# Attentions by two: both older units' value products together behind the scores of the next two

## The reference, cut to what matters

```python
# first block, per head
probs = softmax(concat([scores, sink]))[..., :-1]
out = einsum('bnkgqs,bnskd->bnqkgd', probs, v_band)
# second block: compressed, selected and window attention
p_cmp = where(valid, softmax(where(valid, q @ k_cmp, NEG_INF)), 0.0);  o_cmp = p_cmp @ v_cmp
o_slc = softmax(s) @ v_sel
o_win = softmax(s) @ v_win
return g[0] * o_cmp + g[1] * o_slc + g[2] * o_win
```

## Time and profile before

| | us |
|---|---|
| median of 3 runs | 2228.23 |
| lowest, highest | 2225.65, 2231.48 |
| profiled execution | 2233.68 |
| its span | 2231.9 |
| TensorE busy | 2207.0 (99%) |
| DVE busy | 1552.2 (70%) |
| ACT busy | 1110.0 (50%) |
| GpSimd busy | 198.4 (9%) |
| mean granted clock of TensorE | 0.998 |

### The profile page before, as it was taken

One profiled execution on the slowest core, in us unless ns is written; L12 is line 12 of the kernel. 1 busy time (PEld: TensorE's weight loads), 2 busy tenths in 40 slices (PEclk: granted clock), 3 DMA queues, 4 the chain that ended last, 5 costly groups with the idle time before them and its releaser, 6 DMA issues.

```text
span 2231.9 us, 34104 instructions
## 1 busy us (share of the span) xinstructions
PE 2207.0 (99%) x13650; PEld 1900.3 (85%) x13662; DVE 1552.2 (70%) x2163; ACT 1110.0 (50%) x1719; POOL 198.4 (9%) x191
## 2 busy tenths in 40 slices
PE   8999999999999999999999999999999999999998
PEld 7888888888888888888889988888888888998887
DVE  5777845677864775777787677567666777777764
ACT  4745434655543544445454554455444546355443
POOL 0010200001200110000004011011100000310110
PEclk9999999999999999999999999999999999999999
DMA  7445565445555755554535465565556444355553
GB/s 238 142 142 180 188 200 186 152 133 180 182 193 187 243 189 189 185 182 152 171 105 171 169 215 184 193 236 192 190 184 193 161 164 138 133 199 181 187 189 133
DMA packets 109245, 397.72 MB, mean 178 GB/s; under 512 B 12384, under 2 KB 12528, under 8 KB 108832
## 3 DMA queue, kind: packets, MB, share of 16 engines
q1 hardware_dynamic: 104256, 377.01, 50.8%
q0 software_dynamic: 4832, 18.53, 2.6%
HBM read 395.00 MB, written 1.05 MB: 177 GB/s over the span
## 4 chain that ended last, share of the span: by engine, by line
PE 96%; DVE 2%; ACT 1%; DMA 1%; issue 0%; DVEq 0%; SPq 0%; ACTq 0%; POOLq 0%
PE psum L449 44%; PE psum L600 29%; PE psum L599 15%; PE psum L818 2%; PE psum L963 2%; PE psum L940 1%; PE psum L927 1%; PE psum L898 1%; PE psum L2043 1%; PE psum L1319 0%; DMA ring<-in_weights 0%; DMA pages<-in_gains 0%; PE psum L1333 0%; ACT attn_p L1103 0%; DVE xs L2396 0%
## 5 line engine op out<-in xcount | busy, mean ns | idle before, releaser
L406 DVE TENSOR_TENSOR w_low<-ring,w_high 128x1024 fp32r<-128x1024 f32 x704 | 858.5, 1231 | 332.7 <-ACT w_high L403 331.3
L403 ACT ACTIVATE w_high<-ring 128x1024 fp32r<-128x1024 f32 x704 | 734.6, 1056 | 511.2 <-DMA ring<-in_weights 506.1
L600 PE MATMUL psum<-xT,w_high 128*128 128x512 f32 x2784 | 983.0, 397 | 0.0
L599 PE MATMUL psum<-xT,w_low 128*128 128x256 f32 x2784 | 790.3, 284 | 0.0
L600 PEld LDWEIGHTS psum<-xT,w_high 128*128 128x128 f32 x2784 | 522.8, 188 | 123.5 <-issue 1.0
L599 PEld LDWEIGHTS psum<-xT,w_low 128*128 128x128 f32 x2784 | 526.1, 189 | 3.9 <-issue 1.4
L449 PE MATMUL psum<-w_high,hidden 128*128 128x512 f32 x1216 | 376.9, 390 | 0.0
L449 PEld LDWEIGHTS psum<-w_high,hidden 128*128 128x128 f32 x1216 | 228.3, 188 | 47.2
L449 PE MATMUL psum<-w_low,hidden 128*128 128x512 f32 x608 | 236.6, 389 | 0.0
L449 PE MATMUL psum<-w_high,xT 128*128 128x512 f32 (+2 forms) x640 | 193.3, 382 | 0.7 <-DVE xT L777 0.6
L449 PE MATMUL psum<-rounded_pages,w_high 128*128 128x256 f32 x896 | 165.6, 286 | 0.0
(11 more groups left out here) (238 smaller groups left out, 2089.0 us busy)
## 6 DMA issues: line engine op xcount, KB each, us to landing
ring<-in_weights SPq DMA_DIRECT2D x706, 512.0 KB, 3.5
pages<-in_affine POOLq DMA_DIRECT2D x16, 512.0 KB, 5.5
ring<-in_weights SPq DMA_DIRECT2D x8, 440.0 KB, 3.2
pages<-in_gains POOLq DMA_DIRECT2D x4, 512.0 KB, 4.8
pages<-in_mem POOLq DMA_DIRECT2D x2, 1024.0 KB, 6.6
pages<-in_bias POOLq DMA_DIRECT2D x2, 988.0 KB, 11.8
ring<-in_weights SPq DMA_DIRECT2D x4, 384.0 KB, 3.2
pages<-in_rows POOLq DMA_DIRECT2D x2, 512.0 KB, 5.8
```

Source lines behind the costliest of these rows:

```text
L403: eng.activation(high, raw, ACT.Copy).then_inc(self.flag("w_rounded").sem, 1)
L406: eng.tensor_tensor(self.w_low[:, piece % SLOTS, 0:width], raw, high.bitcast(F32), ALU.subtract).then_inc(self.flag("w_split").sem, 1)
L599: pe.matmul(out[:, 0:SEQ], low, self.xT_high[:, k, :], start=(k == 0), stop=False, skip_group_check=True)
L600: m = pe.matmul(out, high, self.xT[:, k, :, :].rearrange("p x s -> p (x s)"), start=False, stop=(k == kn - 1), skip_group_check=True)
```

## The change

In `attend_tensor_by_two` TensorE's order changes; the other engines' orders do not. Before, the value products of unit i-2 stand behind the scores of units i and i+1, and those of unit i-1 behind the turned weights of unit i. After, both stand behind the scores. At the end, the two last units' value products both stand behind the last two steps' work, in place of one behind each.

```diff
         for i in range(0, len(us), 2):
             self.scores_of_two(pe, l, us[i])
             if i:
-                self.values(pe, l, us[i - 2])
+                for u in us[i - 2:i]:
+                    self.values(pe, l, u)
             between(i)
             self.turn_weights(pe, l, us[i])
-            if i:
-                self.values(pe, l, us[i - 1])
             between(i + 1)
             self.turn_weights(pe, l, us[i + 1])
         for i in range(2):
             between(len(us) + i)
-            self.values(pe, l, us[len(us) - 2 + i])
+        for u in us[-2:]:
+            self.values(pe, l, u)
```

## The result

| | before | after |
|---|---|---|
| median of 7 runs, us | 2226.26 | 2234.09 |
| lowest, highest | 2225.54, 2231.48 | 2232.24, 2237.32 |
| profiled span | 2231.9 | 2232.4 |

The ratio is 1.0032, 95% interval 1.0023 to 1.0041: 7.1 us slower by the ratio, 5.1 to 9.1. The forecast was +4.7, with 2232.9 for the time and 2227.5 to 2239 as its range. It called the loss a small one inside 0.3%; the interval lies on both sides of that bound, so these runs do not settle it.

What follows compares the result with a forecast made beforehand. It took TensorE's queue, 96% of the chain, to bound the kernel. Terms of -3.3 - 0.4 + 5.6 + 2.8 = +4.7 us on the median 2228.23 gave 2232.9 us, range 2227.5 to 2239.

Steps and rivals of the forecast that it cites:

- Step 1: Pairs behind the first: one break less between TensorE's matrix products gains 0.33 us per pair, 3.3 us over 10 pairs.
- Rival D: Pairs and ends: removing the break gains nothing, so 3.7 us of gain vanish; +8.4 us, 2236.6; chance 0.05.
- Step 2: DVE's copies of turned weights: in time in block 1; 0.33 us late in block 2's four branch pairs, cancelling their gain.
- Step 3: End of block 2: two value products together behind two branch products gain 0.2 us per layer, 0.4 in all.
- Step 4: First pair of block 2: V(7) waits for DVE's finish of unit 6; net +3.2 and +2.4, together +5.6 us.
- Step 5: Behind V(7)'s wait in each layer of block 2: TensorE's clock drops, 1.4 us per layer, +2.8 us in all.
- rival B: At the gate and T(8) behind V(7): low clock lasts a second stretch, 1.7 us more per layer; +8.1, 2236.3; chance 0.19.
- Rival A: First pair of block 2: the waits come but the clock holds; +1.9 us, 2230.1; chance 0.17.

Runs made afterwards that it cites:

- only where nothing should be late: Value products joined in block 1, three gate pairs of block 2 and the ends, first and branch pairs unjoined; against the kernel before: 2225.52 against 2228.74 us, ratio 0.9986.
- Short finish: Changed kernel with the last addition of the selected and window attention's finish cut to 8 columns; against the kernel before: 2234.02 against 2228.04 us, ratio 1.0023.
- branch pairs alone: Kernel before with only the two pairs of block 2 beside branch products joined; against the kernel before: 2230.74 against 2228.74 us, ratio 1.0012.
- copy ahead of the rest: Changed kernel, block 2's first pair unjoined, DVE's copy moved ahead of multiplication and weight split from the ninth unit; against the kernel before: 2222.37 against 2228.04 us.
- first pair apart: Changed kernel, but the first pair of block 2 keeps the old order; against the kernel before: 2228.4 against 2228.74 us, ratio 1.0000.
- the filler: Changed kernel with 17 idle matrix products between the value products of units 6 and 7; against the kernel before: 2230.16 against 2228.04 us, ratio 1.0010.
- First pair alone: Kernel before with only the first pair of block 2 joined; against the kernel before: 2238.68 against 2228.74 us, ratio 1.0042.
- second profiles: The kernel before and the changed kernel, both unchanged, each profiled a second time: 2229.59 and 2234.55 us.
- Before again: The kernel before, unchanged, profiled a second time: 2229.59 us.
- after again: The changed kernel, unchanged, profiled a second time: 2234.55 us.
- block 1 alone: Kernel before with only the pairs of block 1 joined; against the kernel before: 2224.6 against 2228.0 us, ratio 0.9985.

## Why the prediction came out as it did

**Right in sign, place and, nearly, size.** The bound, the waiting instruction and its releaser were named, and the time lies in the range. That the total came so near is partly luck, as the last point says. By steps:

- **Step 1, a break: right.** 0.33 per pair predicted. A gate pair of the change (T(9) to T(11), 9.02 us for 9.36) gives 0.34. A pair of block 1 gives 0.4 (T(1) to T(3), 9.30 us for 9.70). Rival D would have it 0. The Trainium skill, TensorE: Matmul & The Clock Gate, Step-by-step: what each phase is for, says that weight loads are pulled ahead of products in flight; if they were pulled across the break too, that would be rival D. These rows speak against it here, as does "only where nothing should be late" with -3.1 (-5.1 to -1.1).
- **Step 2, the copies: the term that failed.** The place was right and the size was not. It stood as 0 for the four branch pairs, "0.33 us, which cancels the gain", with a loss of 0.5 as the worst. It measured +0.85 per pair, +3.4 us, outside those bounds. I took DVE's arrival at the copy from the trace of before, where V(i-1) behind T(i) gave DVE 0.79 us more, and left out the finish. With V(i-1) gone, DVE's list between two copies is the longer one. "Short finish" (waits 0.97 to 0.45) and "branch pairs alone" show it; "copy ahead of the rest" removes it. That DVE would catch up in the wait at V(7) was right, as the 0.80 of "first pair apart" shows.
- **Step 3, the ends:** 0.2 per layer predicted, 0.34 measured (T(19) to L818, 13.21 us for 13.55).
- **Step 4, V(7): right.** A net +3.2 was predicted for layer 0 without the clock. With the filler V(6) to T(9) takes 11.69 us where before took 8.50: +3.2, in layer 1 too. There I had 2.4, 0.8 us too little. In the trace that I read, TensorE was at half clock ahead of V(6) and came late to it while DVE did not, so the finish ended 3.68 us behind the start of V(6) (1870.92 to 1874.60) where it was 4.59 in layer 0; part of the wait was hidden. "First pair alone" and "first pair apart" show the whole to be there.
- **Step 5, the clock: right in kind, 1.5 us too small.** 2.8 predicted, 4.3 measured. In layer 0 3.4 us of full clock are missing, twice the 1.7 of the earlier trace rows, in both profiles of the change. That is what rival B describes, but in one layer only: in layer 1 1.7 are missing. The low clock together costs 4.3, short of the 4.8 at which B would have decided. Rival A falls: the clock is a third to a half of what the first pair costs (1.6 of 4.8 in layer 1, 2.7 of 5.7 in layer 0).
- **Not in the sum:** something outside the attentions gave time back. The rulers say +9.7 (+9.5 in the second profiles), twice the forecast, where the time moved by +7.1 (5.1 to 9.1) and the spans of the second profiles by 4.9. A part of the rest is the faster pace of products of the last section, whose cause is open. So the small miss of the total owes something to two errors of opposite sign.

## What to carry to other kernels

Before two waiting instructions are put together on an in-order engine, check each one's own wait: here one pair's second member also waited for a bank to be emptied, and that pair alone cost more than all the others gained. Two remedies were not tried: the finish of unit 6 ahead of the two maxima in DVE's list, and a second bank for unit 7, which by the timeline would leave a wait of some 1.2 us for its copy (an estimate). When work is taken from between two steps of one engine, the engine that answers has that much less time too: recount its whole list between them instead of reading its old arrival times. And price a wait on TensorE with the clock behind it; 3.6 us of waiting cost another 1.6 to 2.7 us here.

## What I had not expected of the hardware

The same gates run at one of two paces. In 225 to 265 us, the network behind block 1 in layer 0, in which the change alters nothing, TensorE starts 2% more products in the changed kernel. Before, then after (x is the number of products in 40 us):

```profile
225.00:265.00 40.00, 40.00 (x228) 34.67 (x227) 32.42 (x44) 18.59 (x22) 9.52 (x8) 1.00 0.59 184
```
```profile
225.00:265.00 40.00, 40.00 (x233) 35.24 (x232) 33.14 (x47) 18.84 (x22) 10.57 (x8) 1.00 0.59 187
```

Before again has 229, after again and block 1 alone 233. The granted clock is 1.00 in all. In this stage all nine profiles with block 1 joined show the fast pace and all four without it the slow one; it is worth 1.1 us between L818 of layer 0 and the scores of layer 1 (317.81 us for 318.91). In later stages of gates both paces occur too, and there they follow none of the edits: the two kernels before are slow and the two changed ones fast in three stages, and in the last stage the two profiles of the kernel before differ from each other. So the pace is not fixed by the kernel everywhere.

The times of the eight kernels with block 1 joined that were timed lie 0.8 to 3.3 us below what their rulers say; of the two without, one lies 1.1 below and one 0.9 above. The pace can be a part of that, but with intervals of 2 us on either side it is not shown to be all of it. What sets the pace is not settled: "Block 1 alone" shows that its order is enough for the fast pace in this one stage, and no run says why.

In the attentions of block 2, waits of 1.43 to 1.57 us ahead of T(7) never lost the clock in these profiles, one of 2.12 did once, and waits of 3.6 at V(7) did in all eight places where nothing filled them.
